# Selecting one block of experts by pairs of heads during the query projections, with five unit tiles ahead of the gate groups

## The chip, the core and the metric

The kernel runs on one core of one Trainium2 chip. The core has five engines that run side by side and meet at semaphores: TensorE (PE; its weight loads are PEld), VectorE (DVE), ScalarE (ACT), GpSimd (POOL) and SyncE (SP), whose queue starts most of the transfers. The metric is the device time of one execution in microseconds (us).

## The reference, cut to what matters

Two layers of a decoder run for 512 prompt tokens and 32 sample tokens. Each layer has a mixer (attention and a recurrence in layer 0, a convolution in layer 1) and then a retrieval over 16,384 one-neuron experts, which is what the change touches:

```python
q = (xb @ w_q).reshape(blk, PEER_HEADS, 2, PEER_DKH)            # 8 heads, 2 products each
sc = jnp.einsum('nhpd,hpkd->nhpk', q, sub_keys)                 # 128 key scores each
sv, si = lax.top_k(sc, PEER_TOPK)                               # 16 of 128
cand = sv[:, :, 0, :, None] + sv[:, :, 1, None, :]              # sums of pairs
cidx = si[:, :, 0, :, None] * N_KEYS + si[:, :, 1, None, :]
fv, fi = lax.top_k(cand, PEER_TOPK)                             # 16 experts for each head
eidx = jnp.take_along_axis(cidx, fi, axis=-1)
gate = jax.nn.softmax(fv, axis=-1)
act = jax.nn.gelu(jnp.einsum('nd,nhed->nhe', xb, jnp.take(u_tab, eidx, axis=0)), approximate=False)
y = jnp.einsum('nhe,nhed->nd', gate * act, jnp.take(v_tab, eidx, axis=0))
```

## The kernel before

**Dense and lone tokens.** The first 384 tokens, three blocks of 128, are treated densely: all 128 unit tiles (128 experts of `u_tab` each) and all 128 value tiles go through TensorE, and a gate matrix that is zero except for the chosen experts weighs them. The last 128 prompt tokens and the 32 sample tokens are "lone": their rows are gathered one by one.

**Every weight tile** comes as a 512 KB transfer from SP's queue (`load_expert`) into one of four `raw` buffers; ACT copies its high part (`hi`), and DVE subtracts to get the low part (`low`, or POOL in the projections). A unit tile on PE (`units`) is 24 matmuls of 384 columns; ACT then takes the gelu of its result from one of two PSUM halves, so unit tile e starts only after the gelu of tile e-2. Four ring slots hold tiles during the part that matters here.

**The order of one retrieval**, written out by hand on each engine, is this. (1) *Query projections*: 16 tiles `q`; PE projects and scores, DVE takes the best 16 of 128 for four token blocks (`retrieval`), and PE's scores of query q wait until DVE has read those of q-2. A 17th turn of DVE does the sample tokens. (2) *Front*: `FRONT` = 12 unit tiles on PE while DVE selects the first dense block (`select(l, 0, part)`, 15 parts, spread over the tiles by `SEL_QUANTA`). PE then transposes the choice (`choice`). (3) *Gate groups*: 48 groups of 8 tokens, 16 to a block. For each, DVE writes eight one-hot matrices over one axis and five over the other (`onehots`), ACT the other three, PE multiplies them (`gate_group`), and ACT stages the result (`stage_group`). `TILES_AFTER[g]` unit tiles follow group g on PE; 31 are placed so. Meanwhile DVE selects the next block, one part in each group. (4) Five more unit tiles, then values and the remaining units in turn (`AHEAD` = 48 unit tiles come before any value).

**The steps of a tile.** `tile_step(i)` stands for tile i in ACT's and DVE's order: ACT makes the high part of tile i+3 and takes the gelu of tile i-1; DVE makes the low part of tile i+3. On ACT it follows the staging of the group after which the tile stands. On DVE it stands after the one-hots and the selection part of the next group.

**Writing the gates.** The staging buffer holds 8 groups. SP writes it to memory as two transfers of 2 MB (`write_gates`), and the staging of the next 8 groups starts in each half when that half is written. SP's queue is in order:

```python
if 1 <= i <= AHEAD:
    write_units(l, i - 1)          # waits for the gelu of tile i-1
if i + 7 < N_EXP:
    load_expert(l, i + 7)          # waits for the low part of tile i+3
for h in range(ND // 64):
    if i == TILES_BEFORE[8 * h + 7] - 1:
        write_gates(l, h)          # waits for the staging of group 8h+7
```

So a gate write stands behind the load of tile i+7, where i is the last unit tile ahead of group 8h+7.

**At a block's border** DVE's one-hots of the new block wait for `slT`, which ACT copies after PE's `choice`, which PE does after the first unit tile behind the old block's last group.

Of the kernel before, what the change touches and what calls it, by code (L numbers as in the profile page):

```python
# [21 lines left out]
F32 = mybir.dt.float32  # L22
F32R = mybir.dt.float32r
U32 = mybir.dt.uint32
ALU = mybir.AluOpType
# [3 lines left out]
P = 128  # L29
# [35 lines left out]
AHEAD_SLOTS = 4  # L65
GSLOT = 4
# [3 lines left out]
AHEAD, FRONT = 48, 12  # L70
# [72 lines left out]
def ring_slot(t):  # L143

    for t0 in T_EXP:
        if t0 <= t < t0 + AHEAD:
            return (t - t0) % AHEAD_SLOTS
        if t0 <= t < t0 + N_EXP:
            return (t - t0) % SLOTS
    return t % SLOTS  # L150
# [46 lines left out]
def build(nc, xT, stream, utab, vtab, params, consts, mconsts, reset, keysT, kcacheT, vcache, kvcache_n, state_h, convT,  # L197
          yT, kwin_p, vwin_p, hs_p, cb_p, kwin_s, vwin_s, hs_s, cb_s):
    ctx = ExitStack()
    with ctx:  # L200
# [46 lines left out]
        with ExitStack() as z:  # L247
            sb("ring_ahead", [P, AHEAD_SLOTS, 2, D], F32, z)
            stage = sb("stage", [P, NKEY, 64], F32, z)
        zone = sb("zone", [P, SLOTS * 2 * D])  # L250
# [752 lines left out]
        def _(act):  # L1003
# [87 lines left out]
            def experts(l):  # L1091
# [51 lines left out]
                for i in range(FRONT):  # L1143
                    tile_step(i)
                for n in DENSE:
# [7 lines left out]
                    onehots(l, n, 0)  # L1153
                    for q in range(16):
# [235 lines left out]
            act.wait_ge(s_ya, 2 * (KC + 1))  # L1390
            act.dma_start(yT.rearrange("(k p) n -> p k n", p=P), xt[:]).then_inc(s_out, 16)
            act.wait_ge(s_out, 16 * (2 + 4 + 9 + 1))
# [3 lines left out]
        def _(dve):  # L1396
# [43 lines left out]
            def retrieval(l):  # L1440
                norm(1 if l == 0 else 3)
                for q in range(N_WQ + 1):
# [28 lines left out]
                    ch.sync()  # L1471
            def select(l, i, part):
# [3 lines left out]
                done = NTILE * l + i  # L1476
# [3 lines left out]
                if part == 0:  # L1480
                    ch.step(V.tensor_copy(sif[:, 0:2 * H, :], si[:, n, 0:2 * H, :]))
                    for a in range(9):
                        at = CAND_AT[a]
                        if a < 8:
                            w = CAND_W[a]
                            v0, v1 = val[:, :, 0, a:a + 1].to_broadcast([P, H, w]), val[:, :, 1, 0:w]
                            i0, i1 = sidx[:, :, 0, a:a + 1].to_broadcast([P, H, w]), sidx[:, :, 1, 0:w]
                        else:
                            w = 8
                            v0, v1 = val[:, :, 0, 8:16], val[:, :, 1, 0:1].to_broadcast([P, H, 8])  # L1490
                            i0, i1 = sidx[:, :, 0, 8:16], sidx[:, :, 1, 0:1].to_broadcast([P, H, 8])
                        ch.done(V.tensor_tensor(cand[:, 0:H, at:at + w], v1, v0, ALU.add))
                        ch.done(V.scalar_tensor_tensor(out=cidx[:, 0:H, at:at + w], in0=i0, scalar=float(NKEY),
                                                       in1=i1, op0=ALU.mult, op1=ALU.add))
# [11 lines left out]
                elif part == 4:  # L1506
                    if done >= 1:
                        dve.wait_ge(s_ge, done)
                    if i >= 1:
                        dve.wait_ge(s_selT, NDB * l + min(i, NDB))  # L1510
                    V.tensor_tensor(r16[:, 0:H, :], fv[:, 0:H, :], fv[:, 0:H, 0:1].to_broadcast([P, H, 16]),
                                    ALU.subtract).then_inc(s_gx, 1)
# [25 lines left out]
                if part == NPART - 1:  # L1538
                    dve.wait_ge(s_ge, done + 1)
                    ch.step(V.tensor_reduce(r8[:, 0, 0:H], sel[:, 2, 0:H, :], X, ALU.add))  # L1540
                    ch.step(V.reciprocal(r8[:, 1, 0:H], r8[:, 0, 0:H]))
                    out = sel[:, 2, :, :] if n in DENSE else glone[n][:, :].rearrange("p (h r) -> p h r", h=H)
# [572 lines left out]
```

## Time and profile before

| | |
|---|---|
| median of 3 runs | 3564.22 us (3562.22 to 3565.26) |
| profiled execution | 3564.95 us, of which the span of its instructions is 3563.1 us |
| busy over the span | PE 90%, PEld 82%, DVE 76%, ACT 41%, POOL 33% |
| chain that ended last, by engine | PE 72%, DVE 16%, ACT 5%, DMA 4%, issue 3% |
| mean granted clock | 0.951 |

The busy shares are means over stages with different limits. In the rows further down, a timeline row gives the start and the length of an instruction (or of a merged run of equal ones, xN), then engine, line and tiles, and in brackets how long the engine had been idle and what ended that. SPq and ACTq are queues that start transfers. Names of tiles: `oh` one-hots, `slT` the transposed choice, `ring` high and low parts, `ga` gelu, `stage` the gate staging, `pick` the comparison of ranks with candidates.

### The profile page before, as it was taken

What the parts mean: (1) busy time and instruction counts of PE and PEld (TensorE: products, weight loads), DVE (VectorE), ACT (ScalarE), POOL (GpSimd) and SP (SyncE); (2) the same over time, 40 slices, a digit from 0 to 9 for tenths busy, and PEclk for the clock granted to TensorE, in tenths of its full rate; (3) what the DMA queues carried; (4) which work ended last, traced back from release to release, by engine and by line L of the source; (5) the groups of instructions that cost most, each with busy time, mean ns of one, the idle gap of its engine ahead of it and who ended that gap; (6) DMA issues with size and microseconds to landing.
All of it is one profiled execution on the core that took longest, in us unless ns stands there. A gap on an engine that the chain in (4) does not pass through costs nothing.

```text
span 3563.1 us, 48737 instructions
## 1 busy us (share of the span) xinstructions
PE 3212.9 (90%) x18193; PEld 2927.6 (82%) x18193; DVE 2711.5 (76%) x5277; ACT 1474.2 (41%) x2299; POOL 1186.9 (33%) x766
## 2 busy tenths in 40 slices
PE   5885899888799999999987969998879999999998
PEld 5875789888788888888877748988778888888887
DVE  3425457988788888888867874798877888888887
ACT  3443222688633333333323222268873333333332
POOL 2210321000045555555542113200004555555553
PEclk9997699999999999999998989999989999999999
DMA  3110322444499999999962052144439999999997
GB/s 118 50 57 1 95 69 69 146 158 176 157 376 378 363 362 366 358 368 362 361 233 60 24 48 83 60 135 176 170 144 371 379 359 370 357 363 367 360 362 256
DMA packets 424987, 807.81 MB, mean 227 GB/s; under 512 B 233952, under 2 KB 259104, under 8 KB 421280
## 3 DMA queue, kind: packets, MB, share of 16 engines
q1 hardware_dynamic: 318960, 454.23, 38.1%
q0 software_dynamic: 94560, 344.45, 26.0%
q10 hardware_dynamic: 11232, 6.01, 1.3%
q8 instruction: 145, 2.38, 0.3%
q14 instruction: 90, 0.74, 0.1%
HBM read 729.52 MB, written 76.08 MB: 226 GB/s over the span
## 4 chain that ended last, share of the span: by engine, by line
PE 72%; DVE 16%; ACT 5%; DMA 4%; issue 3%; POOL 0%; SPq 0%; DVEq 0%; ACTq 0%; POOLq 0%
PE bank L869 29%; PE bank L857 21%; PE bank L618 14%; DVE cv L1898 2%; DMA gate_matrix<-stage 2%; PE bank L840 2%; DVE ring L1582 2%; DVE oh L1573 1%; DVE oh L1568 1%; DVE pick L1530 1%; PE bank L606 1%; DVE pick L1521 1%; DVE eidx L1537 1%; ACT oh L1066 1%; PE bank L752 1%
## 5 line engine op out<-in xcount | busy, mean ns | idle before, releaser
L857 PE MATMUL bank<-hh,ring 128*128 128x384 f32 x4096 | 1104.6, 342 | 29.0 <-ACT ga L1101 19.6
L1582 DVE TENSOR_TENSOR ring<-raw,ring 128x1024 fp32r<-128x1024 f32 x506 | 617.6, 1223 | 284.6 <-ACT ring L1012 283.9
L869 PE MATMUL bank<-ring,wh 128*128 128x512 f32 x3072 | 828.3, 391 | 0.9 <-DVE wl L1600 0.9
L1951 POOL DMA_INDIRECT rows<-in_utab,gidx x320 | 449.4, 1405 | 1130.2 <-ACT stage L1139 703.3
L857 PEld LDWEIGHTS bank<-hh,ring 128*128 128x128 f32 x4096 | 755.7, 191 | 39.8 <-issue 12.8
L1012 ACT ACTIVATE ring<-raw 128x1024 fp32r<-128x1024 f32 x598 | 622.7, 1053 | 218.3 <-DMA raw<-in_stream 102.7
L857 PE MATMUL bank<-hl,ring 128*128 128x384 f32 x2048 | 693.6, 339 | 0.0
L869 PEld LDWEIGHTS bank<-ring,wh 128*128 128x128 f32 x3072 | 574.4, 188 | 112.3 <-DVE ring L1582 1.2
L1951 POOL DMA_INDIRECT rows<-in_vtab,gidx x320 | 492.3, 1538 | 367.3 <-DVE acc L1622 314.4
L618 PE MATMUL bank<-hh,ring 128*128 128x272 f32 x2752 | 493.9, 299 | 67.4 <-DVE hl L1413 42.8
L1101 ACT ACTIVATE ga<-bank 128x384 f32<-128x384 f32 x256 | 124.7, 487 | 976.3 <-PE bank L857 964.3
L618 PEld LDWEIGHTS bank<-hh,ring 128*128 128x128 f32 x2752 | 408.6, 196 | 81.6 <-issue 50.0
L869 PE MATMUL bank<-ring,wl 128*128 128x512 f32 x1536 | 473.1, 389 | 0.0
L1932 POOL TENSOR_TENSOR ring<-raw,ring 128x1024 fp32r<-128x1024 f32 x92 | 221.9, 2419 | 660.5 <-ACT ring L1012 545.0
L1622 DVE SCALAR_TENSOR_TENSOR acc<-rows,wv,acc 128x1024 f32<-128x1024 f32 x316 | 404.6, 1280 | 11.9
L857 PEld LDWEIGHTS bank<-hl,ring 128*128 128x128 f32 x2048 | 392.2, 191 | 6.1
L1614 DVE CUSTOM_DVE_ANT_0 rows<-rows,htok 128x1024 f32<-128x1024 f32 x320 | 382.1, 1220 | 0.2 <-DMA rows<-in_utab,gidx 0.2
L869 PEld LDWEIGHTS bank<-ring,wl 128*128 128x128 f32 x1536 | 288.3, 188 | 64.1
L840 PE MATMUL bank<-oh 128*128 128x128 f32 x1536 | 215.4, 301 | 102.6 <-DVE oh L1573 87.9
L840 PEld LDWEIGHTS bank<-oh 128*128 128x128 f32 x1536 | 204.3, 213 | 113.2 <-DVE oh L1573 106.0
L618 PE MATMUL bank<-hl,ring 128*128 128x272 f32 x1376 | 293.4, 295 | 0.0
L618 PEld LDWEIGHTS bank<-hl,ring 128*128 128x128 f32 x1376 | 226.2, 196 | 0.0
(299 smaller groups left out, 2963.9 us busy)
## 6 DMA issues: line engine op xcount, KB each, us to landing
raw<-in_stream SPq DMA_DIRECT2D x342, 512.0 KB, 5.4
raw<-in_vtab SPq DMA_DIRECT2D x256, 512.0 KB, 7.8
gate_matrix<-stage SPq DMA_DIRECT2D x24, 2048.0 KB, 9.9
gt<-gate_matrix SPq DMA_DIRECT2D x256, 192.0 KB, 9.5
units_ahead<-ga SPq DMA_DIRECT2D x96, 192.0 KB, 4.1
gv<-units_ahead SPq DMA_DIRECT2D x96, 192.0 KB, 8.8
rows<-in_utab,gidx POOLq DMA_INDIRECT x320, 8.0
rows<-in_vtab,gidx POOLq DMA_INDIRECT x320, 7.9
```

The costliest lines, as they stand in the source:

```text
L618: m = T.matmul(PA[t % 2][:, a, 0:HALF], w[:, ring_slot(t), k * P:(k + 1) * P], h[:, k, a * HALF:(a + 1) * HALF], start=(k == 0 and i == 0) ...
L840: m = T.matmul(PA[e % 2][:, i // 4, (i % 4) * P:(i % 4 + 1) * P], oh2[:, e % 2, i, :], oh1[:, e % 2, i, :], start=True, stop=True)
L857: m = T.matmul(PB[1][:, (e + 1) % 2, 0:ND], w[:, ring_slot(t), k * P:(k + 1) * P], h[:, k, 0:ND], start=(k == 0 and i == 0), stop=(k == KC ...
L869: m = T.matmul(psum[c][:, a, :], w[:, v_n % WSLOT, c * P:(c + 1) * P], v[:, ring_slot(t), 512 * a:512 * a + 512], start=(v_n == 0 and i == ...
L1012: A.activation(ring_hi[:, ring_slot(t), :], raw[b][:], ACT.Copy).then_inc(s_hi, 1)
L1101: A.activation(ga[:, e % ASLOT, :], PB[1][:, (e + 1) % 2, 0:ND], ACT.Gelu).then_inc(s_ga, 1)
L1582: V.tensor_tensor(ring_lo[:, ring_slot(t), :], raw[raw_buffer(t)][:], ring_hi[:, ring_slot(t), :].bitcast(F32), ALU.subtract).then_inc(s_l ...
L1614: V.tensor_tensor_reduce(out=rows[:, slot, :], in0=rows[:, slot, :], in1=htok[b][:, :], scale=1.0, scalar=0.0, op0=ALU.mult, op1=ALU.add, ...
L1622: V.scalar_tensor_tensor(out=acc[b][:, :], in0=rows[:, slot, :], scalar=wv[b][:, j:j + 1], in1=acc[b][:, :], op0=ALU.mult, op1=ALU.add).th ...
L1898: tap = V.scalar_tensor_tensor(out=cv[:, m, 0:NP], in0=up[:, m, i:i + NP], scalar=w, in1=cv[:, m, 0:NP], op0=ALU.mult, op1=ALU.add)
L1932: nc.gpsimd.tensor_tensor(ring_lo[:, slot, :], raw[buf][:], ring_hi[:, slot, :].bitcast(F32), ALU.subtract).then_inc(s_lo, 1)
L1951: nc.gpsimd.indirect_dma_start(out=rows[:, g % ROW_SLOTS, :], out_offset=None, in_=vtab if is_v else utab, in_offset=bass.IndirectOffsetOn ...
```

## The change

- The first dense block is selected by pairs of heads. A new `select_pair(j, part)` has four parts for two heads (candidates; best 16; comparison; product and sum). Pairs 0 to 2 go behind DVE's turns for queries 4 to 15, one part to each turn. Pair 3, `shifted` and `chosen` (which take over lines from `select`) stay in the front. The scratch `pick_pair` needs room, so the query tiles use six ring slots instead of eight (`WQ_SLOTS`).
- `FRONT` goes from 12 to 5; the fifth tile stands behind `choice` on PE, behind the first one-hots on ACT, and behind group 0's one-hots on DVE. `TILES_AFTER` is 1 for every group but ten, so 38 unit tiles stand among the groups. The exponentials of the first block move from ACT's step 3 to step 1 (`EXP_BEFORE`).
- On DVE the low parts of a group's tile stand two groups later instead of one.
- The result goes out in eight transfers of 128 rows, each after its own addition, instead of one.

```diff
+WQ_SLOTS = 6
-AHEAD, FRONT = 48, 12
+AHEAD, FRONT = 48, 5
-TILES_AFTER = [{1: 1, 3: 1, 5: 1, 7: 2}.get(_g % 8, 0) for _g in range(ND // 8)]
-TILES_AFTER[3] = TILES_AFTER[19] = TILES_AFTER[35] = 2
-TILES_AFTER[47] = 0
+NO_TILE = (5, 11, 17, 22, 27, 33, 38, 43, 46, 47)
+TILES_AFTER = [int(_g not in NO_TILE) for _g in range(ND // 8)]
-SEL_QUANTA = [(0,), (1, 2), (3, 4, 5), (6, 7), (8,), (9, 10), (11,), (12, 13), (14,)]
-EXP_BEFORE = {3: 0}
+EXP_BEFORE = {1: 0}
...
-                for i in range(FRONT):
+                for i in range(FRONT - 1):
                     tile_step(i)
...
                     onehots(l, n, 0)
+                    if n == 0:
+                        tile_step(FRONT - 1)
...
-            act.wait_ge(s_ya, 2 * (KC + 1))
-            act.dma_start(yT.rearrange("(k p) n -> p k n", p=P), xt[:]).then_inc(s_out, 16)
+            for k in range(KC):
+                act.wait_ge(s_ya, (KC + 1) + k + 2)
+                act.dma_start(yT[k * P:(k + 1) * P, :], xt[:, k, :]).then_inc(s_out, 16)
...
+                    if 4 <= q < N_WQ:
+                        select_pair(q // 4 - 1, q % 4)
...
+            def select_pair(j, part):
+                n, h0 = SEL_ORDER[0], 2 * j
+                heads = range(h0, h0 + 2)
+                if part == 0:
+                    ch.step(V.tensor_copy(sif[:, 2 * h0:2 * h0 + 4, :], si[:, n, 2 * h0:2 * h0 + 4, :]))
+                    candidates(sv[:, n, 2 * h0:2 * h0 + 4, :].rearrange("p (h s) k -> p h s k", s=2),
...
+                elif part == 2:
+                    ch.step(V.tensor_copy(pos[:, h0:h0 + 2, :], fi[:, h0:h0 + 2, :]))
+                    ch.done(V.tensor_tensor(
+                        pick_pair[:, :, :, :].rearrange("p h r c -> p (h r) c"),
...
+                else:
+                    ch.step(V.tensor_tensor(pick_pair[:, :, :, :], pick_pair[:, :, :, :],
+                                            cidx[:, h0:h0 + 2, :].unsqueeze(2).to_broadcast([P, 2, 16, NCAND]),
+                                            ALU.mult))
+                    ch.done(V.tensor_reduce(eidx[:, h0:h0 + 2, :], pick_pair[:, :, :, :], X, ALU.add))
+                ch.sync()
...
-                for i in range(FRONT):
-                    if i < len(SEL_QUANTA):
-                        for part in SEL_QUANTA[i]:
-                            select(l, 0, part)
+                for i in range(FRONT - 1):
+                    if i == 0:
+                        select_pair(3, 0)
+                        select_pair(3, 1)
+                        shifted(l, 0)
+                    elif i == 1:
+                        select_pair(3, 2)
+                        select_pair(3, 3)
+                        chosen(l, 0)
                     tile_step(i)
                 for n in DENSE:
                     for q in range(16):
                         g = 16 * n + q
                         onehots(l, n, q)
+                        if g == 0:
+                            tile_step(FRONT - 1)
...
-                        if g:
-                            for m in range(TILES_AFTER[g - 1]):
-                                tile_step(TILES_BEFORE[g - 1] + m)
+                        if g >= 2:
+                            for m in range(TILES_AFTER[g - 2]):
+                                tile_step(TILES_BEFORE[g - 2] + m)
```

SP's own code is untouched, but `TILES_BEFORE` moves its gate writes: the last unit tile ahead of groups 7, 15, 23, 31, 39 is 15, 20, 26, 31 and 37 without the change and 10, 17, 23, 30 and 36 with it.

The order on DVE at the border of the first two dense blocks (`slT` is awaited in the row with `selection_T_ready`; `sel` is the old block's last selection step, `ring` a low part, `oh` one-hots). Without the change:

```order
L1550 SCALAR_TENSOR_TENSOR sel<-sel,eidx 128x128 [waits dve_chain]
L1557 MEMSET small 128x1 [waits dve_chain]
L1568 TENSOR_TENSOR oh<-con,slT 128x1024 [waits gate_tokens_done,selection_T_ready]
L1573 TENSOR_SCALAR oh<-con,slT 128x128 x5
L1582 TENSOR_TENSOR ring<-raw,ring 128x1024 [waits hi_ready] x2
L1568 TENSOR_TENSOR oh<-con,slT 128x1024 [waits gate_tokens_done]
```

With it:

```order
L1560 SCALAR_TENSOR_TENSOR sel<-sel,eidx 128x128 [waits dve_chain]
L1567 MEMSET small 128x1 [waits dve_chain]
L1643 TENSOR_TENSOR ring<-raw,ring 128x1024 [waits hi_ready]
L1629 TENSOR_TENSOR oh<-con,slT 128x1024 [waits gate_tokens_done,selection_T_ready]
L1634 TENSOR_SCALAR oh<-con,slT 128x128 x5
L1643 TENSOR_TENSOR ring<-raw,ring 128x1024 [waits hi_ready]
L1629 TENSOR_TENSOR oh<-con,slT 128x1024 [waits gate_tokens_done]
```

The second `ring` row with the change is the low part of tile 20, made in the step of tile 17, which stands behind group 14; it comes after the one-hots that await the new block's choice. Without the change the low part on which SP's second gate write rests, that of tile 23, comes ahead of these rows.

The order on ACT in the front (`sel` the exponentials, `ga` a gelu, `ring` a high part). Without the change:

```order
L1012 ACTIVATE ring<-raw 128x1024 [waits tile_used,raw0_loaded]
L1101 ACT_TABLE_LOAD
L1101 ACTIVATE ga<-bank 128x384 [waits tile_used]
L1012 ACTIVATE ring<-raw 128x1024 [waits tile_used,raw1_loaded]
L1101 ACTIVATE ga<-bank 128x384 [waits tile_used]
L1012 ACTIVATE ring<-raw 128x1024 [waits tile_used,raw2_loaded]
L1089 ACT_TABLE_LOAD
L1089 ACTIVATE sel<-r 128x128 [waits gate_shifted]
L1101 ACT_TABLE_LOAD
L1101 ACTIVATE ga<-bank 128x384 [waits tile_used]
```

With it:

```order
L1017 ACTIVATE ring<-raw 128x1024 [waits tile_used,raw0_loaded]
L1094 ACT_TABLE_LOAD
L1094 ACTIVATE sel<-r 128x128 [waits gate_shifted]
L1106 ACT_TABLE_LOAD
L1106 ACTIVATE ga<-bank 128x384 [waits tile_used]
L1017 ACTIVATE ring<-raw 128x1024 [waits tile_used,raw1_loaded]
L1106 ACTIVATE ga<-bank 128x384 [waits tile_used]
```

The exponentials, which wait for DVE's `shifted`, now stand ahead of the gelu of tile 0 instead of that of tile 2.

## Rows read from the trace of the kernel before

**Rows 1.** Layer 0: length, PE, PEld, DVE, ACT, POOL busy us, PEclk, DMA, GB/s

```profile
485.00:601.00 116.00, 116.00 (x903) 110.90 (x904) 74.74 (x461) 22.39 (x28) 28.75 (x12) 1.00 0.21 65
663.00:965.00 302.00, 243.96 (x1532) 237.53 (x1533) 253.12 (x661) 243.45 (x413) 0.00 (x0) 0.92 0.41 149
```

**Rows 2.** Waits in layer 0's gate groups (663 to 965): us, times, longest

```profile
PE bank L840 <- DVE oh L1573: 45.2, 20, 5.9
DVE ring L1582 <- ACT ring L1012: 34.0, 16, 5.9
```

**Rows 3.** ACT's groups of instructions there: busy us, mean ns | idle before

```profile
L1139 ACT ACTIVATE stage<-bank 128x1024 f32<-128x1024 f32 x42 | 82.8, 1971 | 31.1 <-PE bank L840 31.1
...
L1012 ACT ACTIVATE ring<-raw 128x1024 fp32r<-128x1024 f32 x32 | 34.0, 1062 | 5.1 <-PE bank L857 5.1
L1101 ACT ACTIVATE ga<-bank 128x384 f32<-128x384 f32 x31 | 14.8, 478 | 0.0
```

**Rows 4.** Timeline of DVE: two queries of the projections

```profile
502.25 0.89 DVE L1454 MAX8 sv<-bank 128x8 f32<-128x128 f32 x4 [2.22 <-PE bank L800]
...
509.71 0.89 DVE L1454 MAX8 sv<-bank 128x8 f32<-128x128 f32 x4 [2.15 <-PE bank L800]
```

**Rows 5.** Timeline of DVE selecting the lone sample tokens, which have two heads

```profile
865.50 0.18 DVE L1481 CAST sif<-si 128x64 f32<-128x64 uint32 x1
...
867.29 0.33 DVE L1497 MAX8 fv<-cand 128x8 f32<-128x50 f32 x2
...
878.76 1.82 DVE L1521 TENSOR_TENSOR pick<-pos,con 128x1600 f32<-128x1600 f32 x1
...
887.04 1.81 DVE L1537 TENSOR_REDUCE eidx<-pick 128x32 f32<-128x1600 f32 x1
```

**Rows 6.** Timeline of the front in layer 0: PE, DVE and ACT

```profile
607.96 0.69 PE L857 MATMUL bank<-hh,ring 128*128 128x384 f32 x1 [4.52 <-POOL ring L1932]
615.32 0.29 DVE L1481 CAST sif<-si 128x256 f32<-128x256 uint32 x1
625.26 0.31 ACT L1089 ACTIVATE sel<-r 128x128 f32<-128x128 f32 x1 [0.73 <-DVE r L1511]
...
626.88 0.49 ACT L1101 ACTIVATE ga<-bank 128x384 f32<-128x384 f32 x1
...
659.41 0.28 ACT L1150 ACTIVATE slT<-bank 128x128 f32<-128x128 f32 x1
```

**Rows 7.** Timeline of the gate groups: ACT's stagings, a gate write (SP), a border (DVE)

```profile
665.43 1.98 ACT L1133 ACTIVATE stage<-bank 128x512 f32<-128x512 f32 x2 [1.10 <-PE bank L840]
...
704.51 2.07 ACT L1139 ACTIVATE stage<-bank 128x1024 f32<-128x1024 f32 x1
...
718.50 1.12 ACT L1133 ACTIVATE stage<-bank 128x512 f32<-128x512 f32 x1 [1.81 <-DMA gate_matrix<-stage]
...
753.85 0.32 SPq L440 DMA_DIRECT2D gate_matrix<-stage  x1
...
759.44 1.23 DVE L1568 TENSOR_TENSOR oh<-con,slT 128x1024 f32<-128x1024 f32 x1 [6.79 <-ACT slT L1150]
...
962.93 2.02 ACT L1139 ACTIVATE stage<-bank 128x1024 f32<-128x1024 f32 x1 [7.54 <-PE bank L840]
```

**Rows 8.** Chain of waits: a group and a tile after an idle PE, and without

```profile
728.05 3.79 PE bank L840 x16
731.84 5.14 PE bank L857 x24
736.98 1.80 PE bank L840 x16
...
851.96 4.18 PE bank L857 x24
```

**Rows 9.** Timeline of the end: ACT's queue

```profile
3555.67 0.38 ACTq L1391 DMA_DIRECT2D out_yT<-xt  x1
```

**Rows 10.** The page's transfers: KB each, median us from issue to landing

```profile
units_ahead<-ga SPq DMA_DIRECT2D x96, 192.0 KB, 4.1
```

More of the change, by code:

```diff
@@ L149, in ring_slot @@
             return (t - t0) % SLOTS
+    for t0 in T_WQ:
+        if t0 <= t < t0 + N_WQ:
+            return (t - t0) % WQ_SLOTS
     return t % SLOTS
@@ L249, in build @@
             stage = sb("stage", [P, NKEY, 64], F32, z)
+        with ExitStack() as z:
+            sb("ring_queries", [P, WQ_SLOTS, 2, D], F32, z)
+            pick_pair = sb("pick_pair", [P, 2, 16, NCAND], F32, z)
         zone = sb("zone", [P, SLOTS * 2 * D])
@@ L1471, in retrieval, with candidates @@
                     ch.sync()
+                    if 4 <= q < N_WQ:
+                        select_pair(q // 4 - 1, q % 4)
+            def candidates(val, sidx, h0, H):
+                for a in range(9):
+                    at = CAND_AT[a]
+                    if a < 8:
+                        w = CAND_W[a]
+                        v0, v1 = val[:, :, 0, a:a + 1].to_broadcast([P, H, w]), val[:, :, 1, 0:w]
+                        i0, i1 = sidx[:, :, 0, a:a + 1].to_broadcast([P, H, w]), sidx[:, :, 1, 0:w]
+                    else:
+                        w = 8
+                        v0, v1 = val[:, :, 0, 8:16], val[:, :, 1, 0:1].to_broadcast([P, H, 8])
+                        i0, i1 = sidx[:, :, 0, 8:16], sidx[:, :, 1, 0:1].to_broadcast([P, H, 8])
+                    ch.done(V.tensor_tensor(cand[:, h0:h0 + H, at:at + w], v1, v0, ALU.add))
+                    ch.done(V.scalar_tensor_tensor(out=cidx[:, h0:h0 + H, at:at + w], in0=i0, scalar=float(NKEY),
+                                                   in1=i1, op0=ALU.mult, op1=ALU.add))
@@ L1475, in select @@
                 H = HEADS[n]
-                done = NTILE * l + i
                 val = sv[:, n, 0:2 * H, :].rearrange("p (h s) k -> p h s k", s=2)
@@ L1481, in select @@
                     ch.step(V.tensor_copy(sif[:, 0:2 * H, :], si[:, n, 0:2 * H, :]))
[L1482 to L1494, printed above, removed]
+                    candidates(val, sidx, 0, H)
                 elif part == 1:
@@ L1506, in select @@
                 elif part == 4:
[L1507 to L1512, printed above, removed]
+                    shifted(l, i)
                     for h in range(H):
@@ L1538, in select @@
                 if part == NPART - 1:
[L1539 to L1542, printed above, removed]
[L1543 to L1557 removed]
+                    chosen(l, i)
             def onehots(l, n, q):
@@ L1643, in experts @@
                                 select(l, NDB + part // NPART, part % NPART)
-                        if g:
-                            for m in range(TILES_AFTER[g - 1]):
-                                tile_step(TILES_BEFORE[g - 1] + m)
+                        if g >= 2:
+                            for m in range(TILES_AFTER[g - 2]):
+                                tile_step(TILES_BEFORE[g - 2] + m)
                 n_row = 0
-                for i in range(TILES_BEFORE[-1], N_EXP):
+                for i in range(TILES_BEFORE[-2], N_EXP):
                     tile_step(i)
```

66 lines of the change are left out of this document (50 added, 16 removed).

## The prediction, made blind

> **What bounds the kernel now.** The windows come first, since a busy share over the whole span mixes stages. In the projections PE is busy all the time, DVE 74.7 of 116.0 us [rows 1]: DVE has time to spare, and what is put there is free as long as it fits. In the gate groups no engine is full: PE 244, DVE 253 and ACT 243 of 302 us [rows 1], so the stage is paced by waits between them. The waits name them: PE waited 45.2 us for DVE's one-hots, and DVE 34.0 us for ACT's high parts before it could make a low part [rows 2]; ACT waited 31.1 us for PE's result before it staged a group, and 5.1 us before a high part [rows 3]. That is a ring (staging, high part, low part, one-hots, matmul, staging), and DVE's low part is the link that the change moves by one group. After the groups come five unit tiles and the values in both kernels alike, so a layer is worth what its front and its gate groups give.
>
> **The change, part by part.**
>
> *Pairs of heads in the projections.* A query takes 7.46 us, and DVE stands idle for 2.15 of them, waiting for PE's scores [rows 4]. What a pair costs is not in the trace; the lone sample tokens have two heads as well, with the same shapes. Their candidates took 1.79 us, from 865.50 to 867.29, the comparison's large step 1.82, the reduction 1.81 [rows 5]. With a second large step as long as the reduction and a few short ones, I put the four parts at 1.8, 2.0, 2.1 and 3.7, or 9.6 us in four queries that offer 4 x 2.15 = 8.6. Three pairs make 28.8 us, of which ten idle gaps take 21.5. The rest makes DVE late. PE's scores wait only for the reading of two queries before, so PE isn't held, but DVE comes free some 7.8 us late, at 623.1 in place of 615.3 [rows 6].
>
> *The front.* Tile 0 waits for a bank that is read a little later, so it starts at about 611.9, not 607.96 [rows 6], and tiles 0 and 1 end 2 x 4.2 later [rows 8], at 620.3. Pair 3's first two parts and the shift take DVE from 623.1 to 627.2. Only then can ACT make the exponentials, which now stand ahead of tile 0's gelu. From the start of the exponentials to the end of the gelu behind them passed 2.11 us before (625.26 to 626.88 + 0.49 [rows 6]), so tile 0's gelu ends at 629.3. Tile 2 needs its bank: PE stands idle for 9.0 us. Tile 2 then takes up to 5.1, tile 3 4.2 [rows 8], and with small gaps they end at 639.2; the choice takes 0.5 and its copies 0.8, to 640.5. From there to the end of group 0's staging I take what it took before, 659.69 to 667.41, or 7.7 [rows 6, 7]. That gives 648.3: **19.1 us earlier in each layer**. But 12 - 5 = 7 unit tiles, 7 x 4.18 = 29 us of PE's work [rows 8], are still to be done among the groups.
>
> *The gate groups with 38 tiles in place of 31.* I count from the end of group 0's staging to that of group 47's, 667.41 to 964.95, or 297.5 us [rows 7]. Three things change there.
>
> (a) More steps of ACT. At the five borders of eight groups, ACT waits until the first half of the staging buffer is written (706.58 to 719.62, or 13.1 us, with its half of the next group's staging in it [rows 7]), and the steps of the tiles behind the border's group lie in that wait. Before, ten of the 31 stood there; now five of the 38. So 33 steps stand in the open and not 21. A step is a high part and a gelu, 1.06 + 0.48 [rows 3], of which some 0.2 overlaps with the neighbours: 12 x 1.3 = **+15.6**.
>
> (b) Later gate writes at blocks' borders. Before, the write followed the staging of group 15 at once, at 753.85, while DVE's next one-hots waited for the new choice until 759.44 [rows 7]. Now SP's load in front of that write waits for a low part that stands behind those one-hots. One tile fewer behind group 15 brings the copies, and with them the one-hots, some 1.5 us forward, to 757.9; one-hots take 2.5 and the low part 1.2, so the write goes at 761.6, or 7.8 us late. Two such borders: **+15.6**. Below this it is nothing, if the low part comes before the one-hots have to wait; more than that it can hardly be.
>
> (c) The ring is cut. With the low part a group later, DVE need no longer wait for a high part that was only just ordered. The most that this can give back is ACT's idle time for PE, 31.1 + 5.1 = 36.2 [rows 3]; the least is nothing, since DVE gets 7 more low parts. Two things in those 36.2 us are not the ring's. PE restarts slowly behind each of the five borders: a group took 3.79 and not 1.80, a tile 5.14 and not 4.18 [rows 8], or 3.0 together, 15.0 for five. And the last staging waited 7.5 [rows 7], in the block in which DVE still selects the lone tokens. I take the rest, 36.2 - 15.0 - 7.5: **-13.7**.
>
> Sum of the stage: +15.6 + 15.6 - 13.7 = +17.5. With the front: -19.1 + 17.5 = -1.6 in a layer. Layer 1 runs the same order; taken alike, -3.2 in both.
>
> *The smaller edits.* Six query slots in place of eight: nothing, as PE's own pace hides the loads (DMA share 0.21 [rows 1]); without that cover a late tile would cost PE its wait.
>
> *The result in eight transfers.* The one transfer of 2.2 MB was issued at 3555.67 [rows 9], and the span ends at 3563.1, 7.4 us later. Now seven of eight pieces leave while DVE still adds, and the last, 272 KB, goes at the same time. A 192 KB transfer took 4.1 us from issue to landing [rows 10]; at that the end comes **3.3 us earlier**. At worst it is nothing, if the pieces queue behind one another.
>
> The Trainium skill (DMA: Bandwidth & Descriptors, Bandwidth) speaks against this edit: it asks for transfers of at least 1 MiB to reach three quarters of the peak rate. By that the eight small pieces would gain nothing, and the sum below would be 3561.7; no transfer here shows it for a result in pieces.
>
> **Sum.** 3564.95 - 3.2 - 3.3 = 3558.4. The profiled execution lies 0.7 us above the median of 3564.22; I say 3558 on the median's scale. A measurement of this kernel tells 0.2%, or 7.1 us, from no change: 3557.1 to 3571.3 would be "same".
>
> **Rivals.**
>
> *Forecast: the groups give back what the front gains,* 3548 to 3570.
>
> *Faster: the gate writes aren't late.* If ACT's staging runs behind DVE, so that the low part is done before the border, (b) falls away in four places, 31 us: 3527. For it: the low part is only one step behind. Against it: DVE stood idle for 6.79 us at this border [rows 7], so it was ahead there, and its order is fixed.
>
> *Faster still: the ring was all of ACT's idle time.* Then (c) gives 36.2 and each layer 24 us: 3513. Against it: slow restarts are seen in the chain [rows 8] and stay.
>
> *Slower: the ring isn't cut but fed.* DVE was the busiest engine of the stage with 253 of 302 us [rows 1], and 7 low parts and the steps' waits come on top, while PE's 244 grow by 29. If PE waits for one-hots as long as before, (c) is nothing and each layer 13.7 us longer: 3586. It decides (over 3571.3) when less than half of the 13.7 comes back.
>
> *The change doesn't do what it says:* if the pairs made DVE so late that PE's scores waited for it, the front's gain would shrink by what PE waits. A read two queries behind leaves 2 x 7.46 us of room, which the 7.8 us don't fill, so I give it no chance of its own.
>
> **How the numbers follow.** Forecast 0.43, writes not late 0.17, ring wholly cut 0.15, ring fed 0.25. Of the forecast's own range about four tenths lie below 3557.1. Faster: 0.17 + 0.15 + 0.17 = 0.49. Slower: 0.25 less a few cases that stay under 3571.3, so 0.23. Same: 0.28. The range leaves out most of the ring wholly cut and the upper part of the ring fed: 3525 to 3581.
>
> **What would show it.** Staging of group 0 some 19 us earlier in each layer; PE idle for about 9 us between tiles 1 and 2 of the front; DVE free some 8 us later after the queries. In the groups: the writes behind groups 15 and 31 issued some 8 us after the staging, and DVE's 34.0 us of waiting for high parts mostly gone. If these waits are gone and PE's for one-hots are not, the slower rival holds. The last landing should come 3 us sooner after the last addition. The prediction is wrong if staging 0 to staging 47 takes well under 310 us or well over 320.

## The result, and the profile after

| | before | changed |
|---|---|---|
| median | 3563.22 us (3560.59 to 3565.26, 4 runs) | 3591.65 us (3590.1 to 3595.09, 4 runs) |
| profiled span | 3563.1 us | 3590.9 us |
| mean granted clock | 0.951 | 0.942 |
| PE, DVE, ACT busy over the span | 90%, 76%, 41% | 89%, 76%, 41% |

The changed kernel is slower by 0.8%: ratio 1.0084, 95% interval 1.0068 to 1.01. That is outside the range on record (3525 to 3581), and on the side that was given 0.23.

First the timeline of ACT's stagings, with the columns of [rows 7]: those of groups 0, 7, 15 and 47 in layer 0, and of groups 0 and 47 in layer 1. Behind them stand the latter two in the kernel before.

```profile
653.16 2.02 ACT L1138 ACTIVATE stage<-bank 128x512 f32<-128x512 f32 x2
...
694.74 2.01 ACT L1144 ACTIVATE stage<-bank 128x1024 f32<-128x1024 f32 x1
...
745.74 2.01 ACT L1144 ACTIVATE stage<-bank 128x1024 f32<-128x1024 f32 x1 [1.75 <-PE bank L845]
...
975.71 2.07 ACT L1144 ACTIVATE stage<-bank 128x1024 f32<-128x1024 f32 x1 [4.46 <-PE bank L845]
...
2370.92 2.02 ACT L1138 ACTIVATE stage<-bank 128x512 f32<-128x512 f32 x2
...
2692.62 2.06 ACT L1144 ACTIVATE stage<-bank 128x1024 f32<-128x1024 f32 x1 [4.44 <-PE bank L845]
```

```profile
2367.88 1.97 ACT L1133 ACTIVATE stage<-bank 128x512 f32<-128x512 f32 x2 [1.07 <-PE bank L840]
...
2662.20 2.02 ACT L1139 ACTIVATE stage<-bank 128x1024 f32<-128x1024 f32 x1 [6.57 <-PE bank L840]
```

Staging 0 ends at 655.2 in place of 667.4 [rows 7]: 12.2 us earlier, not 19.1. From there to the end of staging 47, at 977.8, pass 322.6 us in place of 297.5, or 25.1 more. Layer 1 repeats it: staging 0 comes 9.7 us sooner after layer 0's last staging than in the kernel before, and its groups take 321.7 in place of 294.4, or 27.3 more. Now the stretch from staging 0 to staging 47 in layer 0, with the columns of [rows 1], before and changed, and then the waits in it, with those of [rows 2], three of the kernel before and four of the changed one:

```profile
667.41:964.95 297.54, 240.20 (x1503) 233.96 (x1502) 248.74 (x641) 240.13 (x407) 0.00 (x0) 0.92 0.41 147
...
655.18:977.78 322.60, 263.38 (x1669) 260.50 (x1669) 257.52 (x657) 251.24 (x422) 0.00 (x0) 0.91 0.43 149
```

```profile
ACT stage L1133 <- DMA gate_matrix<-stage: 12.1, 5, 3.5
...
PE bank L840 <- ACT oh L1066: 7.1, 2, 4.6
PE bank L857 <- ACT ga L1101: 6.4, 4, 2.9
```

```profile
ACT stage L1138 <- DMA gate_matrix<-stage: 48.6, 10, 9.3
...
PE bank L862 <- ACT ga L1106: 27.3, 7, 7.4
...
PE bank L845 <- ACT oh L1071: 21.0, 2, 10.9
...
PE bank L845 <- DVE oh L1634: 9.7, 3, 3.4
```

PE has its seven tiles more in the groups: 263.4 us of work and 240.2 before. Its waits for DVE's one-hots have mostly gone, 9.7 us in place of 45.2 [rows 2], as the cut ring should do. Yet PE is idle for as long as before, 59.2 us of the stretch and 57.3 before, since other waits have come: 27.3 us for gelus in place of 6.4, and 21.0 for ACT's one-hots in place of 7.1. Both are made by ACT, which waits 48.6 us for gate writes, in ten waits; it was 12.1 before. The changed kernel's chain of waits at the border behind group 15 (start, length, what) tells why:

```profile
749.87 0.34 PE bank L831 x3
...
750.76 0.29 ACT slT L1155
...
751.07 1.23 DVE oh L1629
752.29 1.28 DVE oh L1634 x5
753.57 1.15 DVE ring L1643
...
754.73 0.33 SPq L440
...
755.11 1.01 SPq L445
...
756.16 12.54 DMA gate_matrix<-stage
```

It is the path that term (b) spoke of: choice, its copies, one-hots, low part, then SP's load, and only then the gate write at 755.11, 7.4 us after staging 15 ended at 747.75. The write before went out at once [rows 7]. What the late write does to PE stands in the timelines of ACT and PE:

```profile
768.72 1.03 ACT L1138 ACTIVATE stage<-bank 128x512 f32<-128x512 f32 x1 [3.55 <-DMA gate_matrix<-stage]
771.87 1.26 ACT L1071 ACTIVATE oh<-dist,slT 128x128 f32<-128x128 f32 x3
773.24 3.75 PE L845 MATMUL bank<-oh 128*128 128x128 f32 x16 [10.10 <-ACT oh L1071]
```

ACT's one-hots for the next group stand behind the staging that waits, and PE stands for them for 10.1 us.

The front, in the timelines of PE, DVE and ACT (the last row is of layer 1):

```profile
610.31 3.90 DVE L1523 TENSOR_TENSOR pick_pair<-pos,con 128x1600 f32<-128x1600 f32 x1
617.54 0.66 PE L862 MATMUL bank<-hh,ring 128*128 128x384 f32 x1 [11.76 <-DVE sc L1467]
628.63 0.20 DVE L1504 CAST sif<-si 128x64 f32<-128x64 uint32 x1
632.80 0.31 ACT L1094 ACTIVATE sel<-r 128x128 f32<-128x128 f32 x1 [5.56 <-DVE r L1542]
635.06 0.66 PE L862 MATMUL bank<-hh,ring 128*128 128x384 f32 x1 [6.11 <-ACT ga L1106]
...
2280.94 2.39 DVE L1496 SCALAR_TENSOR_TENSOR cidx<-sif 128x16 f32<-128x16 f32 x1
```

Tile 0 starts at 617.5 (611.9 forecast), DVE comes to pair 3 at 628.6 (623.1), the exponentials stand at 632.8 (627.2), and PE waits 6.1 us ahead of tile 2 (9.0). Of these delays 2.3 us were there when the queries began (DVE's first scores at 497.1 and at 494.7 before); between 170 and 200 us PE ran at a granted clock of 0.83 in this execution and of 0.91 in the one before. The rest is below.

The tail did what was said:

```profile
3582.75 4.87 DVE L1733 TENSOR_TENSOR xt<-xt,bank 128x512 f32<-128x512 f32 x8 [0.56 <-PE bank L915]
3583.47 4.52 ACTq L1399 DMA_DIRECT2D out_yT<-xt  x8
```

The last addition ends at 3587.6 and the span at 3590.9, 3.3 us later; before, the span ended 7.5 us after the last addition and 7.4 after the issue [rows 9].

### The profile page after: what moved, and what is told of

Its sections match the earlier page's. It is cut to its first block, busy times and chain, and to the rows that moved or that the text cites. A ratio compares the mean times of both kernels' runs of the same rounds, so it can differ in the third digit from the quotient of the medians.

```text
span 3590.9 us, 48870 instructions
## 1 busy us (share of the span) xinstructions
PE 3212.2 (89%) x18193; PEld 2934.5 (82%) x18193; DVE 2735.6 (76%) x5403; ACT 1471.0 (41%) x2297; POOL 1189.8 (33%) x766
## 4 chain that ended last, share of the span: by engine, by line
PE 74%; DVE 14%; DMA 5%; ACT 4%; issue 2%; POOL 0%; SPq 0%; DVEq 0%; ACTq 0%; POOLq 0%
PE bank L874 29%; PE bank L862 26%; PE bank L623 11%; DMA gate_matrix<-stage 4%; PE bank L845 3%; DVE cv L1966 2%; DMA units_ahead<-ga 1%; PE bank L611 1%; PE bank L757 1%; DVE si L1465 1%; DVE si L1478 1%; PE bank L773 1%; DMA raw<-in_stream 1%; DVE sc L1467 1%; DVE sv L1462 1%
## 5 line engine op out<-in xcount | busy, mean ns | idle before, releaser
L862 PE MATMUL bank<-hh,ring 128*128 128x384 f32 x4096 | 1118.0, 345 | 102.2 <-ACT ga L1106 76.4
L845 PE MATMUL bank<-oh 128*128 128x128 f32 x1536 | 202.3, 290 | 64.4 <-ACT oh L1071 42.5
```

The lines of the kernel that those rows point to most:

```text
L845: m = T.matmul(PA[e % 2][:, i // 4, (i % 4) * P:(i % 4 + 1) * P], oh2[:, e % 2, i, :], oh1[:, e % 2, i, :], start=True, stop=True)
L862: m = T.matmul(PB[1][:, (e + 1) % 2, 0:ND], w[:, ring_slot(t), k * P:(k + 1) * P], h[:, k, 0:ND], start=(k == 0 and i == 0), stop=(k == KC ...
```

## The experiments

Each kernel is timed against the kernel before; the changed kernel's own 3592 is the time to compare the variants with. "s0 to s47" is the time from the end of staging 0 to that of staging 47, read as above, for layers 0 and 1.

| kernel | median us | ratio to before, 95% interval | s0 to s47, us |
|---|---|---|---|
| before | 3563 to 3565 | | 297.5, 294.4 |
| changed | 3591.65 | 1.0084 [1.0068, 1.01] | 322.6, 321.7 |
| e1: write first | 3553.73 | 0.9972 [0.9962, 0.9982] | 304.4, 300.8 |
| e12: low parts one group behind again | 3569.36 | 1.0016 [1.0007, 1.0025] | 314.6, 313.8 |
| e2: front of 12 again | 3585.14 | 1.0059 [1.0045, 1.0072] | 289.8, 290.0 |
| e3: before + later low parts | 3548.51 | 0.9962 [0.9948, 0.9975] | 285.2, 283.3 |
| e4: before + eight transfers | 3557.89 | 0.9988 [0.9979, 0.9998] | 297.9, 292.4 |
| e5: before + both | 3546.54 | 0.9941 [0.9928, 0.9955] | 289.4, 286.0 |
| e6: e1 + two tiles at borders | 3521.96 | 0.9875 [0.986, 0.989] | 288.7, 288.4 |
| e11: e6 without write first | 3566.63 | 1.0005 [0.9996, 1.0014] | 310.5, 308.7 |
| e7: e1 + front of 7 | 3546.82 | 0.9951 [0.9937, 0.9964] | 297.3, 298.5 |
| e8: e1 + pairs a query sooner | 3543.52 | 0.9938 [0.9925, 0.9952] | 303.7, 301.2 |
| e9: e6 + e8 | 3513.99 | 0.9866 [0.985, 0.9882] | 289.2, 288.1 |
| e10: e9 + front of 7 | 3513.6 | 0.9863 [0.9847, 0.9879] | 286.0, 283.6 |

**e1: the write ahead of the load.**

```diff
+                    for h in range(ND // 64):
+                        if i == TILES_BEFORE[8 * h + 7] - 1:
+                            write_gates(l, h)
                     if i + 7 < N_EXP:
                         load_expert(l, i + 7)
-                    for h in range(ND // 64):
-                        if i == TILES_BEFORE[8 * h + 7] - 1:
-                            write_gates(l, h)
```

> The changed kernel, with SP's gate write put ahead of the load of tile i+7 instead of behind it. Theory A (the late gate writes at the two borders between dense blocks are a cost of their own): the writes behind groups 15 and 31 are issued right at the end of their staging, 7 to 8 us sooner, and the four of them in both layers give 28 to 32 us: about 3561. Theory B (PE paces the groups with seven tiles more, and a write that comes sooner only lets PE stand elsewhere): under 10 us, 3582 to 3591.

Measured: 3553.7, or 38 us less than the changed kernel. Theory A holds, and the price is above what the delay alone makes. SP's timeline shows the write at once after the staging:

```profile
747.92 0.80 SPq L445 DMA_DIRECT2D gate_matrix<-stage  x2
```

Four writes, 7.3 to 8.0 us sooner each, brought 38 us, 9.5 each: the two legs from staging 15 to 23 and from 31 to 39 went from 60.9 and 61.9 us to 53.2 and 50.8 in layer 0, and to 50.3 and 50.9 from 61.5 twice in layer 1. The others stayed within 0.5 us. So the cost of the late writes sits in just these legs. PE's two waits for ACT's one-hots, 21.0 us, are gone in e1.

**e12: the low parts back.** `if g >= 2` and `g - 2` become `if g` and `g - 1` in DVE's loop over the groups, as before the change.

> The changed kernel with the low parts one group behind their tile again, nothing else. The low part that the write rests on then stands ahead of the border's one-hots, so the writes behind groups 15 and 31 go out at the end of their staging (39 us less than 3592), and the gain of the later low parts is lost (12 us in each layer, as on the kernel before): 3573 to 3581. If the writes stay late: 3600 or more. If the later low parts gave nothing with 38 tiles: 3554.

Measured: 3569.4, a little under the first range. The legs behind groups 15 and 31 fall to 55.0 and 52.5 in layer 0, so the writes are on time here too. What made them late is thus two edits together: a tile behind group 14, and a low part two groups behind it, which falls behind the border's one-hots. The table before had no tile behind group 14, so with it (e3) the same later low parts make no write at these borders more than 0.7 us late. e12 against e1 also prices the later low parts in the changed layout, with writes on time in both: 10.2 us in layer 0 and 13.0 in layer 1. The waits in e12's groups of layer 0 show PE waiting for one-hots again:

```profile
PE bank L845 <- DVE oh L1634: 28.6, 13, 5.1
```

**e2: the front of 12 tiles and its table.**

```diff
-AHEAD, FRONT = 48, 5
+AHEAD, FRONT = 48, 12
-NO_TILE = (5, 11, 17, 22, 27, 33, 38, 43, 46, 47)
-TILES_AFTER = [int(_g not in NO_TILE) for _g in range(ND // 8)]
+TILES_AFTER = [{1: 1, 3: 1, 5: 1, 7: 2}.get(_g % 8, 0) for _g in range(ND // 8)]
+TILES_AFTER[3] = TILES_AFTER[19] = TILES_AFTER[35] = 2
+TILES_AFTER[47] = 0
```

> The changed kernel with 12 front tiles and the 31 tiles among the groups as before; pairs, later low parts, earlier exponentials and eight transfers stay. Theory A: the groups go back to 290 to 298 us from staging 0 to staging 47, but the front keeps PE's longer waits of the changed kernel (12 us ahead of tile 0, 6 us ahead of tile 2), so staging 0 comes 10 to 14 us later than in the kernel before; with 4 us from the transfers, about 3575 to 3588. Theory B (the seven tiles among the groups are what costs): it is at least as fast as the kernel before, 3550 to 3564.

Measured: 3585.1, as theory A has it. Staging 0 ends at 678.7, 11.3 us later than before. With 12 tiles the old selection was hidden behind them, so the pairs, with the exponentials that the change moved ahead of tile 0's gelu, are a loss there: PE waits 11.8 us ahead of tile 0 and 6.5 ahead of tile 2. They pay only if the front gets shorter. What each of the two edits costs there was not run alone.

**e3: the later low parts alone, on the kernel before.** The same loop over `g - 2` as in the change.

> The kernel before, with DVE's low parts two groups behind their tile instead of one, nothing else. The term (c) of the prediction: DVE's 34 us of waiting for high parts go, and 14 to 36 us in each layer with them: 3492 to 3537. Rival (the ring's waits are hidden behind the wait for the gate write and come back there): within 7 us of the kernel before, 3557 to 3571.

Measured: 3548.5, 14 us less, so neither range holds it. The groups are 12.3 and 11.1 us shorter: term (c) exists, near the 13.7 that was taken. But some of it is given back where the prediction saw both kernels alike, behind the last group. The timeline of PE there, and PE's first value:

```profile
972.13 0.66 PE L857 MATMUL bank<-hh,ring 128*128 128x384 f32 x1 [5.49 <-ACT ga L1101]
...
987.55 1.09 PE L869 MATMUL bank<-ring,wh 128*128 128x512 f32 x4
```

PE waits 5.5 us for a gelu ahead of a unit tile, and the first value comes 36.5 us behind staging 47 (which ended at 951.0); in layer 1 34.4. In the kernel before it was 31.6 both times, with a wait of 2.9 there. Low parts that stand two groups behind are still to be made when the groups end, and SP's loads and writes, queued behind them, go out beside or behind the last gate write. In the timelines of ACT the gelu itself waits for the writing of units to memory (`units_ahead`), here and in the kernel before:

```profile
971.50 0.49 ACT L1101 ACTIVATE ga<-bank 128x384 f32<-128x384 f32 x1 [7.86 <-DMA units_ahead<-ga]
```

```profile
981.79 0.49 ACT L1101 ACTIVATE ga<-bank 128x384 f32<-128x384 f32 x1 [5.25 <-DMA units_ahead<-ga]
```

Between staging 47 and that gelu SP issues four weight loads in e3 and three in the kernel before. (That is read from the traces; no run changed it alone.)

**e4: the eight transfers alone, on the kernel before; e5: both.** The diff of e4 is the change's own on ACT's last lines; e5 adds e3's.

> The kernel before, with the result in eight transfers, nothing else. The changed kernel's trace ends 3.3 us after the last addition, the one before 7.5: 4 us less, about 3559. Rival (the pieces queue behind one another, and the difference in the traces is chance): no change, 3563.

> The kernel before, with the low parts two groups behind their tile and the result in eight transfers; no pairs, 12 front tiles. If the two gains lie in different stages they add: 14 us from the low parts and 5 from the transfers, about 3543 to 3545. If they are the same slack met twice: 3548.

Measured: 3557.9 for e4, 5 us less. For e5 3546.5, between its two forecasts: its interval takes in both 3543 and 3548, so whether the gains add in full is open.

**e6: two tiles behind the borders' groups, on top of e1.**

```diff
-NO_TILE = (5, 11, 17, 22, 27, 33, 38, 43, 46, 47)
+NO_TILE = (3, 5, 11, 13, 17, 19, 22, 25, 27, 29, 35, 38, 43, 46, 47)
 TILES_AFTER = [int(_g not in NO_TILE) for _g in range(ND // 8)]
+for _g in (7, 15, 23, 31, 39):
+    TILES_AFTER[_g] = 2
```

> The changed kernel with SP's gate write ahead of the load, and two tiles instead of one behind groups 7, 15, 23, 31 and 39; the 38 tiles stay 38, five other groups lose theirs. Theory A (term (a): a tile's steps that lie in the wait for the gate write are free, those that don't cost 1.3 us of ACT or 4.2 us of PE each): 5 steps in each layer, 13 to 40 us less than with the write first alone (3554), so 3514 to 3541. Rival (PE paces the stage wherever its tiles stand, and a second tile behind a border only puts off the choice of the next block): 3549 to 3560.

Measured: 3522.0, 32 us less than e1, with the same 38 tiles. The timelines of ACT and PE behind group 7 in the changed kernel, where the write is on time as in e1, show a place where this was lost:

```profile
703.92 1.06 ACT L1138 ACTIVATE stage<-bank 128x512 f32<-128x512 f32 x1 [3.77 <-DMA gate_matrix<-stage]
709.91 1.02 ACT L1138 ACTIVATE stage<-bank 128x512 f32<-128x512 f32 x1 [4.93 <-DMA gate_matrix<-stage]
710.74 1.05 ACT L1017 ACTIVATE ring<-raw 128x1024 fp32r<-128x1024 f32 x1
711.68 0.48 ACT L1106 ACTIVATE ga<-bank 128x384 f32<-128x384 f32 x1
712.31 0.66 PE L862 MATMUL bank<-hh,ring 128*128 128x384 f32 x1 [7.37 <-ACT ga L1106]
```

ACT works in order. The gelu that PE's next tile needs stands behind the staging that waits for the write, so PE stands for 7.4 us; that tile then takes 6.0 us where one in a running row took 4.2. With two tiles behind the border's group a second gelu stands ahead of that staging. In e6 PE's waits for a gelu around this border are 0.9 and 1.4 us, the longer one here:

```profile
707.24 0.42 PE L864 MATMUL bank<-hh,ring 128*128 128x384 f32 x1 [1.43 <-ACT ga L1108]
```

In all the groups of layer 0 PE waits 27.7 us for gelus in e1 and 17.4 in e6. The windows from staging 0 to staging 47 of e1 and of e6 show both halves of the gain:

```profile
655.50:959.90 304.40, 261.77 (x1667) 258.88 (x1666) 257.13 (x657) 251.13 (x421) 0.00 (x0) 0.93 0.45 158
```

```profile
653.40:942.10 288.70, 254.91 (x1668) 250.28 (x1667) 256.59 (x657) 249.78 (x421) 0.00 (x0) 0.97 0.47 167
```

For the same work PE is busy 6.9 us less, at a granted clock of 0.97 of full speed and not 0.93, and idle 8.8 us less (42.6 to 33.8). The table also takes a tile from six other groups and gives one to a seventh. In the two legs that hold as many tiles in both kernels, from staging 7 to 23, e6 is 8.1 us shorter in layer 0 and 3.2 in layer 1; so the second gelu at the border and the tiles' new places are not told apart here.

**e11: e6 with the late writes.** Only the table of e6; SP as in the change.

> The changed kernel with two tiles behind groups 7, 15, 23, 31 and 39 and SP's order as it was, so the writes behind groups 15 and 31 still stand behind a load whose low part follows the next block's first one-hots. If a late write costs what it cost before (39 us with it, 3592, against 3554 without), about 3560. If the second tile behind the border covers the later landing: 3524 to 3540.

Measured: 3566.6, 45 us more than e6. A second tile does not cover a late write (8.4 us late here); the first theory holds.

**e7: a front of seven tiles, on top of e1.**

```diff
-AHEAD, FRONT = 48, 5
+AHEAD, FRONT = 48, 7
-NO_TILE = (5, 11, 17, 22, 27, 33, 38, 43, 46, 47)
+NO_TILE = (5, 11, 13, 17, 22, 27, 29, 33, 38, 43, 46, 47)
-EXP_BEFORE = {1: 0}
+EXP_BEFORE = {3: 0}
...
                     elif i == 1:
                         select_pair(3, 2)
+                    elif i == 2:
                         select_pair(3, 3)
+                    elif i == 3:
                         chosen(l, 0)
```

> The changed kernel with SP's gate write ahead of the load, and the front of seven tiles (36 among the groups), with the exponentials back in ACT's step 3 and pair 3's steps spread over DVE's steps 0 to 3. Theory (PE's wait of 6 us ahead of tile 2 comes from the gelu of tile 0, which stands behind the exponentials on ACT): the wait ahead of tile 2 goes, two more tiles are done by nearly the same time, and the groups get 5 to 9 us shorter in each layer: 3536 to 3544. Rival (the front is DVE's, and PE only waits elsewhere): 3550 to 3556.

Measured: 3546.8, 7 us less than e1, half of what was expected. PE's wait ahead of tile 2 is gone in e7, so the theory names the wait rightly; but PE now waits 2.15 us ahead of tile 3, for DVE's low part, so DVE's order takes part of the gain.

**e8: the pairs one query sooner, on top of e1.**

```diff
-                    if 4 <= q < N_WQ:
-                        select_pair(q // 4 - 1, q % 4)
+                    if 3 <= q < N_WQ - 1:
+                        select_pair((q - 3) // 4, (q - 3) % 4)
```

> The changed kernel with SP's gate write ahead of the load, and the parts of pairs 0 to 2 one query sooner (from query 3). One more idle gap of 2.15 us is used, and the comparison of pair 2, 3.9 instead of 1.8 us long while GpSimd ran its three subtractions, falls ahead of them. If GpSimd's work is what stretched it, it takes 1.8 us and DVE is free 4 to 5 us sooner: 8 to 10 us less than 3554 over both layers, 3544 to 3546. If not, it stays 3.9 us long and the gain is 2 us a layer: 3550.

Measured: 3543.5, 10 us less than e1. The timelines of e1 and of e8 (DVE's pair 2, and GpSimd's subtractions beside it):

```profile
608.47 8.53 POOL L2000 TENSOR_TENSOR ring<-raw,ring 128x1024 fp32r<-128x1024 f32 x3 [40.14 <-ACT ring L1017]
609.85 1.01 DVE L1522 CAST pos<-fi 128x32 f32<-128x32 uint32 x1
610.89 3.91 DVE L1523 TENSOR_TENSOR pick_pair<-pos,con 128x1600 f32<-128x1600 f32 x1
```

```profile
605.92 8.53 POOL L2000 TENSOR_TENSOR ring<-raw,ring 128x1024 fp32r<-128x1024 f32 x3 [40.18 <-ACT ring L1017]
599.85 0.18 DVE L1522 CAST pos<-fi 128x32 f32<-128x32 uint32 x1
600.06 1.83 DVE L1523 TENSOR_TENSOR pick_pair<-pos,con 128x1600 f32<-128x1600 f32 x1
607.25 2.69 DVE L1528 TENSOR_TENSOR pick_pair<-pick_pair,cidx 128x1600 f32<-128x1600 f32 x1
609.98 1.82 DVE L1531 TENSOR_REDUCE eidx<-pick_pair 128x32 f32<-128x1600 f32 x1
```

Out of GpSimd's way the cast takes 0.18 and not 1.01 us, and the comparison 1.83 and not 3.91. The multiplication, which now falls beside GpSimd, takes 2.69 and not its 1.83, the reduction its usual 1.82.

**e9 and e10: the gains together.** e9 is e6 with e8's lines; e10 is e9 with e7's front, 36 tiles among the groups, two of them behind each border's group.

> The changed kernel with the gate write ahead of the load, two tiles behind the borders' groups and the pairs one query sooner. The front and the groups are stages behind one another, so the gains should add: 3522 less 10, 3510 to 3514. If the earlier front only runs into the same waits: 3522.

> As e9_border_sooner, with the front of seven tiles, the exponentials in ACT's step 3 and pair 3 spread over DVE's steps 0 to 3; 36 tiles among the groups. If the seven-tile front still gives its 7 us: 3503 to 3508. If PE's wait ahead of tile 2, already down to 3.7 us with the pairs sooner, was what it gained from: 3508 to 3514.

Measured: 3514.0 and 3513.6. e9's gains add. In e10 the seven-tile front gives nothing more, as its second case had it: the pairs sooner had already cut the wait ahead of tile 2 to 3.9 us in e9; e10 has none there, and 0.6 ahead of tile 4. e9 and e10 are 1.3 to 1.4% faster than the kernel before, and 78 us faster than the changed one.

## Why the prediction was wrong

The terms of a layer can now each be read: (a) is e12 less before, (b) the changed kernel less e1, (c) e1 less e12, all from staging 0 to staging 47; the last line is the time from staging 47 to PE's first value, 34.4 and 34.2 us in the changed kernel. Layer 1's front is the 9.7 us of above with the 2.8 that layer 0 lost behind its groups.

| term, us in a layer | predicted | layer 0 | layer 1 |
|---|---|---|---|
| front, to the end of staging 0 | -19.1 | -12.2 | -12.5 |
| (a) 38 tiles in place of 31 | +15.6 | +17.1 | +19.4 |
| (b) late gate writes at blocks' borders | +15.6 | +18.2 | +20.9 |
| (c) the ring is cut | -13.7 | -10.2 | -13.0 |
| behind the groups | 0 | +2.8 | +2.6 |
| sum | -1.6 | +15.7 | +17.4 |

With the tail, -4.2 in place of -3.3 (7.5 to 3.3 us after the last addition), this makes 28.9 us, against 27.8 between the two spans. The groups' sum itself, 25.1 and 27.3 us, was put at 17.5. All four terms have the sign they were given and stand where they were put; but every one was sized in the change's favour, in a sum of large terms that nearly cancelled, and a fifth was taken for nothing.

- **The front, the largest miss, 7 us a layer.** The step that failed is "Three pairs make 28.8 us, of which ten idle gaps take 21.5 [...] DVE comes free some 7.8 us late": the price of a pair, 9.6 us, was taken from a stretch in which GpSimd stood still. In layer 0 pair 2's comparison runs beside GpSimd's low parts and takes 3.9 us, its cast 1.0: 2.9 us more, on the path to tile 0, to pair 3, and to the exponentials. In layer 1 the cast takes 1.75 us, the comparison 3.9, and a step of pair 1's candidates, also beside a low part of GpSimd's, 2.39 in place of 0.17: 5.9 us more. e8 took pair 2's comparison off the path and gained 10 us in two layers, one idle gap of 2.15 us in each included. Of layer 0's miss, another 2.3 us was there when the queries began, and tile 2, behind PE's wait, took 6.9 us where 5.1 was taken. That this wait was 6.1 and not 9.0 us is slow work too: tiles 0 and 1, behind a wait of 11.8 us, took 11.4 us and not 8.4. (The sum quoted has a slip: 28.8 less 21.5 is 7.3, not 7.8.)
- **(a), 1.5 and 3.8 us too low, and for another reason than was given.** The text counted ACT's time for steps outside the border's wait (a wait that it puts at 13.1 us; from 706.58 to 719.62 are 13.0). e6 shows that where the tiles stand counts more than their number: its 38 tiles take 288.7 and 288.4 us, no more than the 31 of e2 (289.8 and 290.0), which has the same later low parts and writes at most 0.7 us late. They fill time in which PE was idle, 48.4 us in e2 and 33.8 in e6 in layer 0. Against e1, with the tiles where the change put them, e6's stage lost 15.7 and 12.4 us. A table with two tiles at each border, as the kernel before has it, was the cover, and the new table took it away.
- **(b), 2.6 and 5.3 too low.** The forecast lateness of 7.8 us was measured at 7.4; but the legs grew by 7.7 in one case and by 10.6 to 11.2 in three. Of the 18.2 and 20.9 us between the changed kernel and e1, 16.6 and 19.5 are idle time of PE, which stands for ACT's one-hots behind the late staging, and 1.6 and 1.4 are PE's work. So "more than that it can hardly be" was wrong; why three legs grew by 3 to 4 us more than the write was late is open.
- **(c) held,** on both kernels: 10.2 and 13.0 in the changed one, 12.3 and 11.1 in e3. But the sign that was to show it was badly chosen: DVE's waits for high parts did not go (36.6 us in nine waits of the groups); they no longer stand ahead of one-hots that PE needs. PE's waits for DVE's one-hots went.
- **Behind the groups.** "After the groups come five unit tiles and the values in both kernels alike" failed: the instructions are alike, what SP has in its queue beside the last gate write is not. e12, with the low parts one group behind, has its first value 31.4 and 31.5 us behind staging 47, so the later low parts are what costs the 2.6 to 2.8 us (3.3 to 3.9 between e12 and e1). The order against the gate write is not the cause: with the write first (e1) the value comes 35.3 and 34.8 us behind staging 47. In the changed kernel and e1, as in e3, SP issues four weight loads ahead of the awaited gelu of layer 0, and in e12, as in the kernel before, three; in e1 ACT waits 9.9 us for a load just ahead of that gelu. That the fourth load is what costs is likely, not shown.
- **The eight transfers** gave 4.2 us in the trace and 5 alone (e4). The Trainium skill (DMA: Bandwidth & Descriptors, Bandwidth) asks for transfers of at least 1 MiB for three quarters of the peak rate; here eight of 272 KB ended 3.3 us after the last addition and one of 2.2 MB 7.5 us after it, so the time left after the last addition decided.
- **The rivals.** The slower one forecast 3586 and came closest, by a mechanism that the runs rule out: it had PE waiting for DVE's one-hots as long as before, and these waits fell from 45.2 to 9.7 us, while term (c) came back on both kernels. "The gate writes aren't late" was e1's kernel, and e1 gained 38 us, not 31.

Not settled: whether the one load more behind the last group is what holds up that gelu, and how much of e6's 32 us is the slower PE and how much the wait itself, since the two come together.

## What to carry to other kernels

A transfer that frees a buffer should not stand behind a load in an in-order queue when that load waits for work on the far side of the same border; moving one instruction on another engine by a group, together with a new place for a tile, put it there, and the diff of the queue shows nothing. When work is taken out of a stretch that waits for a transfer, look for what it covered: here two tiles at each border, the second one's gelu ahead of the waiting staging, kept the matrix engine running. And where a sum's terms are ten times its result, price each term from rows with the same neighbours running, and let the range take the terms' errors with one sign.

## What the hardware showed beyond expectation

DVE and GpSimd take turns, by kind of instruction. Beside GpSimd's subtractions of two SBUF operands, DVE's comparison of two SBUF operands took 3.9 us in place of 1.83, its multiplication 2.69, and its cast of 32 columns 1.0 in place of 0.18; a reduction with one operand took its usual 1.82. In the changed kernel's layer 0 the cast ends at 610.27, with GpSimd's first subtraction (610.24), and the comparison at 614.21, 1.7 us behind the second (612.53). GpSimd's third, on record from 612.49, takes 3.92 us where one alone takes 2.4, and ends 2.2 behind the comparison:

```profile
612.49 3.92 POOL L2000 TENSOR_TENSOR ring<-raw,ring 128x1024 fp32r<-128x1024 f32 x1
```

So each of these waits until the other engine's instruction has ended. In layer 1, where all three subtractions started ahead of the comparison, GpSimd's took 6.96 us together and only DVE was held up; in layer 0 they took 8.53, in the kernel before 7.02. The Trainium skill (SBUF — State Buffer, SBUF: two separate sides) states that the two engines share one pair of ports, locked for a whole instruction, and that DVE contends there in its two-port modes, or when it has two SBUF inputs against a GpSimd operation that reads SBUF; these times agree with a lock for a whole instruction. In which mode the cast, with its one operand, ran is not in the trace.

PE's own work isn't of fixed length: the same work of layer 0's gate groups kept PE busy for 261.8 us in e1 at a granted clock of 0.93, and for 254.9 us in e6 at 0.97, with the idle time cut from 42.6 to 33.8 us. The idle time alone does not set it: in e11, with e6's tiles and the late writes, PE is idle for 53.4 us and busy for 257.1, at 0.94.
